# A hybrid attention and state-space layer on one core: running sums, a group's first weights and the first tile's factor moved forward, output weight sums moved a root on

## The reference, cut to what matters

```python
h    = rms_norm(x, pre_norm_w) * (1 + scale) + shift
proj = h @ w_in                        # split: q, k, v, g, gate_lr | z, xbc, dt_raw
o    = gla_chunked(q, k, v, log_a)     # 4 heads, S_t = diag(a_t) S_{t-1} + k_t^T v_t
o    = rms_norm(o, gla_norm_w) * silu(g)
xbc  = silu(causal_depthwise_conv(xbc, conv_w, conv_b))
y    = ssd_chunked(xs, dt, A, Bm, Cm)  # 2 groups of 8 heads, decay from cumsum(dt * A)
y    = rms_norm((y + d_skip * xs) * silu(z), ssd_norm_w)
out  = x + gate * rms_norm(concat(o, y) @ w_out, post_norm_w)
```

## Time and profile before

| what | value |
|---|---|
| median of 3 runs | 1660.09 us (1658.78 to 1662.48) |
| profiled execution, its own time | 1662.56 us |
| its span | 1660.8 us |
| granted TensorE clock, mean over the span | 0.992 of full speed |
| busy share | PE 97%, PEld 83%, DVE 63%, ACT 51%, POOL 24% |
| DMA | 231.14 MB, mean 139 GB/s |

### The profile page before, as it was taken

One profiled execution on the slowest core, in us unless ns is written; L12 is line 12 of the kernel. 1 busy time (PEld: TensorE's weight loads), 2 busy tenths in 40 slices (PEclk: granted clock), 3 DMA queues, 4 the chain that ended last, 5 costly groups with the idle time before them and its releaser, 6 DMA issues. The chain is left out here.

```text
span 1660.8 us, 27425 instructions
## 1 busy us (share of the span) xinstructions
PE 1607.6 (97%) x9990; PEld 1386.1 (83%) x9990; DVE 1047.0 (63%) x1752; ACT 842.2 (51%) x1498; POOL 400.5 (24%) x449
## 2 busy tenths in 40 slices
PE   5999999999999999998999999999999999999997
PEld 4788888888788888897888887888888878888886
DVE  5545454465444644466777768777777844785986
ACT  5765565555444554464545555554445554334332
POOL 2301110112222222210232222232322220451423
PEclk9999999999999999999999999999999999999999
DMA  9523442354534533433222225332222336675886
GB/s 326 149 84 116 135 122 72 101 175 141 184 127 145 173 117 128 146 96 126 73 77 71 81 69 171 100 111 72 76 76 70 122 108 205 237 243 162 308 272 199
DMA packets 131358, 231.14 MB, mean 139 GB/s; under 512 B 9907, under 2 KB 81859, under 8 KB 126134
## 3 DMA queue, kind: packets, MB, share of 16 engines
q1 hardware_dynamic: 123910, 190.76, 35.8%
q10 hardware_dynamic: 6512, 38.80, 6.3%
q0 software_dynamic: 832, 0.22, 0.3%
HBM read 177.05 MB, written 52.70 MB: 138 GB/s over the span
## 5 line engine op out<-in xcount | busy, mean ns | idle before, releaser
L1164 PE MATMUL ps<-hl,w 128*128 128x512 f32 x1488 | 374.3, 401 | 0.5 <-ACT qk L618 0.5
L1164 PEld LDWEIGHTS ps<-hl,w 128*128 128x128 f32 x1488 | 275.1, 189 | 56.8 <-issue 1.8
L1884 PE MATMUL ps<-hl,w 128*128 128x256 f32 x2304 | 294.1, 287 | 0.1
L1884 PEld LDWEIGHTS ps<-hl,w 128*128 128x128 f32 x2304 | 281.4, 192 | 8.2 <-issue 7.9
L1170 PE MATMUL ps<-w,hl 128*128 128x256 f32 x1536 | 200.8, 287 | 0.4 <-DVE w L859 0.4
L1170 PEld LDWEIGHTS ps<-w,hl 128*128 128x128 f32 x1536 | 190.5, 191 | 3.0 <-DVE w L859 0.8
L1750 DVE SCALAR_TENSOR_TENSOR c_acc<-c_before,conv_col,c_acc 128x256 f32<-128x256 f32 x288 | 158.7, 553 | 47.0 <-ACT c_acc L1618 40.1
L1888 PE MATMUL ps<-hl 128*128 128x512 f32 x768 | 180.7, 395 | 4.9 <-DVE hl L1719 4.9
L1888 PEld LDWEIGHTS ps<-hl 128*128 128x128 f32 x768 | 144.5, 190 | 34.8 <-DVE hl L1719 5.1
L2273 PE MATMUL ps<-w,hl 128*128 128x512 f32 x720 | 164.2, 389 | 0.2 <-DVE hl L2209 0.2
L2273 PEld LDWEIGHTS ps<-w,hl 128*128 128x128 f32 x720 | 135.0, 188 | 28.5 <-issue 0.6
(11 more groups left out here) (248 smaller groups left out, 2646.2 us busy)
## 6 DMA issues: line engine op xcount, KB each, us to landing
x_sb<-h SPq DMA_DIRECT2D x52, 512.0 KB, 4.3
w_raw<-in_w_in SPq DMA_DIRECT2D x44, 512.0 KB, 5.4
c_ac<-step_sums ACTq DMA_DIRECT2D x16, 1024.0 KB, 4.8
d_a_raw<-mixed_in SPq DMA_DIRECT2D x29, 512.0 KB, 4.0
c_h_raw<-h SPq DMA_DIRECT2D x56, 256.0 KB, 2.8
d_a_raw<-mixed_in SPq DMA_DIRECT2D x11, 1024.0 KB, 5.0
w_sums<-late ACTq DMA_DIRECT2D x8, 1280.0 KB
w_raw<-w_sums SPq DMA_DIRECT2D x40, 256.0 KB, 3.8
```

Of the source, the lines that this page charges most:

```text
L1164: mm = pe.matmul(ps[:, PROJ + u % 2, :], w[:, u, k, a, :], hl[:, par, k, b, :], start=(k == 0 and i == 0), stop=(k == KT - 1 and i == 2))
L1884: mm = pe.matmul(ps[:, PROJ + u % 2, 0:B2], w[:, u, k, a, :], hl[:, par, k, b, :], start=(k == 0 and i == 0), stop=(k == KT - 1 and i == 2))
```

## The change

1. Attention, sums: of the five `out_sum` of a strip, three now stand behind the factor of tile 2 and two behind that of tile 3 (before: behind tiles 1 and 2; in step 8 all five behind tile 2). Loads and stores of strips move one or two slots on in ScalarE's queue. The second `again_lows` of a step moves from slot 4 to slot 6.
2. Start of the recurrence: the first `load_ac` is issued in ScalarE's queue before the attention's last part, once the last `products` are made; the first h loads go behind the loads of the last two z columns and the last attention store in SP's queue. For this the SBUF order of the recurrence's tensors changes, with a filler `c_gap`, and GpSimd waits for the last attention outputs before it clears `before`.
3. A group's first two weight columns are loaded in step 1 of the group before instead of in its last step.
4. GpSimd makes the factor of a step's first tile ahead of the second tile's `skip`, not behind it.
5. The first of the `first_products` waits for all units but the last; the fifth waits for that one.

```diff
             def _(act):
-                attention[2](act)
-                recurrence[2](act)
+                attention[2](act, 0)
+                recurrence[2](act, 0)
+                attention[2](act, 1)
+                recurrence[2](act, 1)
                 projection[2](act)
...
-    AGAIN_SLOTS = (3, 4, 9, 10)
+    AGAIN_SLOTS = (3, 6, 9, 10)
...
                         if n == SUMS_AT:
-                            for i in ((), (0, 1, 2, 3, 4), ())[t - 1]:
+                            for i in ((), (0, 1, 2), (3, 4))[t - 1]:
                                 out_sum(1, i)
                         elif SUMS_AT < n < SUMS_AT + KT - 1:
-                            for i in ((0, 1, 2), (3, 4), ())[t - 1]:
+                            for i in ((), (0, 1, 2), (3, 4))[t - 1]:
                                 out_sum(n - SUMS_AT + 1, i)
...
-                    if n == SUMS_AT and i == 5:
+                    if n == SUMS_AT and i == 6:
                         load_quarters(1)
-                    if SUMS_AT < n < SUMS_AT + KT - 1 and i == 2:
+                    if SUMS_AT < n < SUMS_AT + KT - 1 and i == 4:
                         load_quarters(n - SUMS_AT + 1)
-                    if SUMS_AT < n < SUMS_AT + KT and i == 0:
+                    if SUMS_AT < n < SUMS_AT + KT and i == 1:
                         store_sums(n - SUMS_AT)
...
-        before = sb("c_before", [P, UCONV, HIST + B2])
...
         z = sb("c_z", [P, 2, TB2, GW])
+        yt = sb("c_yt", [P, TB2, GW])
+        btok = sb("c_btok", [P, NS])
+        ms = sb("c_ms", [P, TB2])
+        mse = sb("c_mse", [P, TB2])
+        rstd = sb("c_rstd", [P, TB2])
+        neg_half = sb("c_neg_half", [P, 1])
+        gap = sb("c_gap", [P, 96])
         ac = sb("c_ac", [P, HG, B2])
+        before = sb("c_before", [P, UCONV, HIST + B2])
...
-                sp.wait_ge(handed["att_ready"], handed["last_att"])
-                for q in range(QS):
-                    load_h(2, 2, 0, q)
                 return
             if part == 1:
                 for u in (UZ + 2, UZ + 3):
                     load_w(0, u)
+                sp.wait_ge(handed["att_ready"], handed["last_att"])
+                for q in range(QS):
+                    load_h(2, 2, 0, q)
                 return
...
+                if isinstance(s, int) and s == 1:
+                    for u in (0, 1):
+                        load_w(g + 1, u)
                 if group_ends:
-                    for u in (0, 1, 2):
-                        load_w(g + 1, u)
+                    load_w(g + 1, 2)
...
             pool.memset(past[:, :], 0.0).then_inc(consts_ready, 1)
+            pool.wait_ge(handed["o_done"], handed["last_o"])
             pool.memset(before[:, :, 0:HIST], 0.0).then_inc(consts_ready, 1)
...
                     decay_state(r, g, t)
+                    if t == TB2 - 1:
+                        rstd_of(r, 0)
                     skip(r, t)
-                for t in range(TB2):
-                    rstd_of(r, t)
+                rstd_of(r, TB2 - 1)
...
-            load_ac(0, 0, 0)
+            if piece == 0:
+                act.wait_ge(handed["prod_ready"], handed["last_prod"])
+                load_ac(0, 0, 0)
+                return
...
                 if u == 0:
+                    pe.wait_ge(unit_out, G * S * UP - 1)
+                    pe.wait_ge(h_ready, (G * S - 1) * QS)
+                if u == 4:
                     pe.wait_ge(unit_out, G * S * UP)
-                    pe.wait_ge(h_ready, (G * S - 1) * QS)
```

More of the change, by code:

```diff
@@ L535, in gpsimd, with scalar @@
             pool.wait_ge(late_cols_loaded, 16 * (TAPS + 3))
-        def scalar(act):
+        def scalar(act, piece):
             def x_square(b, t):
@@ L750, in step @@
                         again_high(m, H_SLOTS.index(i))
[L752 to L774, removed]
-                high(0, k)
-                high(0, k + 1)
@@ L777, in scalar, with main @@
-            w_high(0, 2)
-            for t in range(TB):
-                x_square(1, t)
-            code_part(0)
-            evacuate(0, 0)
-            evacuate(0, 1)
-            code_high(0)
-            act.wait_ge(xrstd_ready, 2)
-            for t in range(2, TB):
-                act.activation(x_sb[:, t, :], x_sb[:, t, :], ACT.Copy, scale=x_rstd[:, t:t + 1]).then_inc(xn_ready, 1)
-            w_high(0, 3)
-            for n in range(STEPS):
-                step(n)
+            def main():
+                act.wait_ge(c_loaded, 16)
+                act.activation(c_act[:, :], c_col[:, :], ACT.Silu).then_inc(c_ready, 1)
+                act.preload_act_table_set("natural_log_exp_and_others")
+                for t in range(TB):
+                    x_square(0, t)
+                act.wait_ge(loads, 64)
+                act.wait_ge(consts_ready, 9)
+                act.activation(wg[:, :, 0:RC], wg_raw[:, :, :], ACT.Copy).then_inc(gate_w_hi, 1)
+                act.wait_ge(consts_ready, 10)
+                act.activation(w2[0:RANK, :], w2_raw[:, :], ACT.Copy).then_inc(gate_w_hi, 1)
+                act.activation(w2[R0:R0 + RANK, :], w2_raw[:, :], ACT.Copy).then_inc(gate_w_hi, 1)
+                act.wait_ge(xrstd_ready, 1)
+                for t in range(TB):
+                    act.activation(x_sb[:, t, :], x_sb[:, t, :], ACT.Copy, scale=x_rstd[:, t:t + 1]).then_inc(xn_ready, 1)
+                for k in range(KT):
+                    first_copy(k)
+                w_high(0, 0)
+                w_high(0, 1)
+                for k in range(0, KT, 2):
+                    act.wait_ge(gain_ready, k // HK + 1)
+                    if k == 0:
+                        act.wait_ge(first_raw, KT)
+                    even_full(0, k, first_full[:, k, :])
+                    high(0, k)
+                    high(0, k + 1)
+                w_high(0, 2)
+                for t in range(TB):
+                    x_square(1, t)
+                code_part(0)
+                evacuate(0, 0)
+                evacuate(0, 1)
+                code_high(0)
+                act.wait_ge(xrstd_ready, 2)
+                for t in range(2, TB):
+                    act.activation(x_sb[:, t, :], x_sb[:, t, :], ACT.Copy, scale=x_rstd[:, t:t + 1]).then_inc(xn_ready, 1)
+                w_high(0, 3)
+                for n in range(STEPS):
+                    step(n)
@@ L791, in scalar @@
+            if piece == 0:
+                main()
+                return
             m = (STEPS - 1) * TB
@@ L1386, in ssd @@
         xend = sb("c_xend", [P, HG, SP_])
-        btok = sb("c_btok", [P, NS])
         state = sb("c_state", [P, HG, SP_])
```

8 lines of the change are left out of this document (2 added, 6 removed).

## The result

| | before | changed |
|---|---|---|
| median, first comparison | 1660.74 us (4 runs) | 1643.07 us (4 runs, 1641.83 to 1644.33) |
| ratio, 95% interval | | 0.989 (0.9878 to 0.9902) |
| profiled execution, its span | 1662.56, 1660.8 us | 1642.21, 1640.5 us |
| TensorE busy | 1607.6 us | 1602.4 us |

The kernel is 17.7 us faster (16.3 to 20.3 by the interval of the ratio); the forecast was 1643.0 us.

The account below looks back on a forecast made before the run. TensorE, busy 97% of the span, was taken as the bound, so only its idle time could be won. Terms 7.0 + 5.7 + 2.1 + 2.1 + 0.2 = 17.1 us gave a median of 1643.0 us, range 1639.5 to 1647.

Parts of the forecast that it names:

- Sums, 7.0 us: Attention steps 8, 11 and 12: moving sums, loads and stores removes TensorE waits, 7.0 us won, bounds 2.3 and 8.7.
- The 8.0 us taken as removable: Attention: waits of 1.56, 1.79 and twice 1.54 us, plus 1.59 us of slower matmuls in step 8, could go.
- The give-back, taken as 1.0 us: Attention, seven steps: two sums now run beside the products that the next step's scores wait for; 1.0 us taken off.
- The choice of the row over the rule's price: Sums beside products: the profile's 1.03 us per sum, 2.06 for two, preferred to the skill's exclusion for the whole instruction.
- The rival's price: Sums and products exclude each other: two sums of 1.50 us hold products 3.0 us, giving 1647.8 us; chance 0.15.
- The start of the recurrence, 5.7 us: Start of the recurrence: z columns land sooner, winning 3.6 us of wait and 2.13 of slow clock; bounds 2.0 and 7.0.
- The group's first columns, 2.1 us: Last step of group 0: early column loads win 2.9 us, less 0.8 for the clock; bounds 0.5 and 5.7.
- The give-back by the clock, taken as 0.8 us: Group 0's last step: 0.8 us taken off for a slow clock behind the new wait at the turn.
- the first rival, no new wait: Group 0's last turn: the fifth column comes sooner, so early columns bring 5.7 us, giving 1639.4 us; chance 0.12.
- The first tile's factor, 2.1 us: First step of group 1: with the factor ahead of the second skip, TensorE's whole wait of 2.1 us goes.
- the rival of a late skip in 16 steps: All 16 recurrence steps: the factor ahead delays the second skip, costing 20.6 us, giving 1663.6 us; chance 0.03.
- The first products, nothing: Behind the last step: the 1.46 us wait at the first products moves to the next block, nothing is won.

Follow-up runs that it names:

- the changed kernel again: The changed kernel measured once more without an edit, in a later comparison with the kernel before: 1643.37 us against 1661.40, ratio 0.9895.
- scaling the tile first: Against the changed kernel, ScalarE scales the first tile ahead of its split of the fifth column in group 0's last step: 1642.11 us, ratio 0.9888.

## Why the prediction was right, point by point

- **Sums, 7.0 us: right in sum, its halves not.** Undone they cost 7.0 us by medians; by the two profiles, with the slow clock of step 8, they brought 8.9. The 8.0 us taken as removable held 1.59 us of that clock, which is there only sometimes. Without it 6.4 us were to go, and 7.4 went (7.1 and the 0.3 given back); the rest is not traced to single waits. The give-back, taken as 1.0 us, was 0.3. That the halves made up for each other is luck. The choice of the row over the rule's price held: 2.06 us by the row, 2.2 measured, room 2.18. But row and rule were one mechanism, not two. In the scan of the earlier trace rows three of the four instructions took 1.40 to 1.45 us instead of 0.4, one per sum, as one product per sum is 1.1 us longer now. A sum that runs alone takes 1.30 us (three in 3.91). The Trainium skill, SBUF — State Buffer, section "Who interferes with whom", says that a VectorE instruction with two inputs in SBUF and a GpSimd instruction that reads SBUF do not run at the same time; the trace agrees but for some 0.2 us a pair (1.77 us, where 1.30 and 0.68 one after the other are 1.98). The rival's price was wrong, not its mechanism: 1.50 us was the length of a sum that had itself stood for VectorE.
- **The start of the recurrence, 5.7 us: right, a little short.** By the profiles 6.5: 4.4 of the wait (3.6 predicted; 3.6 to 4.4 in the eleven executions with the new order) and 2.1 of the clock. Undone in halves: 5.2 and 1.8 by medians, 5.5 and 1.1 in the traces. The new order of the SBUF tensors, which the early load needs, was not undone.
- **The group's first columns, 2.1 us: right.** A new wait of about 3 us at the turn was named, 2.58 came. By the profiles 1.8 us; undone, 2.0 by medians. The give-back by the clock, taken as 0.8 us, was 1.1 to 1.6 in four executions of this step and nothing in five: near their mean, but the price of none of them. Of the first rival, no new wait, nothing was seen.
- **The first tile's factor, 2.1 us: right.** The stretch gained 2.3 us; the rival of a late skip in 16 steps shows nowhere. VectorE's waits for GpSimd's skip at c_yt are 10.7 us in 12 places against 10.3 in 12 before, 0.9 us at most in both.
- **The first products, nothing: right.** The wait moved and is 1.62 us, predicted 1.7. It ends with c_btok, which stands right behind the weighted decay in VectorE's queue.

Undone one by one the parts cost 7.0 + 5.2 + 1.8 + 2.0 + 2.7 - 0.9 = 17.8 us by the medians; the whole is 18.0 us in the comparison of the changed kernel again. In the traces they cost 7.1 + 5.5 + 1.1 + 1.6 + 3.9 + 0.0 = 19.2 us, and the profiles stand 20.3 apart. With each term uncertain by 1 to 2 us this shows that no part of several us hid behind another, and not more. That the forecast met the first median within 0.1 us is luck in part: by the two profiles the terms were 3.2 us short (17.1 of 20.3), 1.9 of them in the sums, and the profiled execution of before was 1.8 us above its median.

## What to carry to other kernels

Follow a late operand back through the queue in which it stands, and look at what comes next on that engine: part 5 moved its wait and won nothing, and scaling the tile first kept 1.7 of 4.3 us, most of the 1.7 by the clock, each time because the next operand was nearly as late. Before work is moved beside other work, compare the room there with how much it will stretch the instructions there (1.1 us per sum), not with a length that it showed beside something else (1.50 us). And a wait's cost by the clock should be booked as a chance, from several executions.

## What the runs showed of the hardware that was not expected

A wait of 2.1 us was followed by 48 matmuls of 11.17 us in one execution and of 12.77 in another; a wait of 3.04 us by 11.15. The granted clock after a wait is not read from the wait's length.

A column of 512 KB took 4.0 to 4.1 us from issue to landing in eleven executions, 5.4 with 1 MB of plain loads issued 6.3 to 3.7 us ahead of it, and 6.2 with 1 MB as broadcast to 128 partitions issued 5.4 us ahead. That the broadcast makes the difference is not shown: there is one execution of each, and the two were not issued at the same distance.
